# A four-layer transformer kernel on one core: the first tile's turnings moved ahead of the last output products at the layer boundaries

## The reference

```python
# first block (layers 0, 1): a norm behind the part too
x = x + gt[:, None, :] * rmsnorm(o, g_post)
h = modulate(rmsnorm(x, g_pre), shift, scale)     # h * (1 + scale) + shift
# second block (layers 2, 3)
h = h + g1 * y
a = rmsnorm_2(h, norm) * (1.0 + sc) + sh
```

## Time and profile before

| | us |
|---|---|
| three runs, median (lowest, highest) | 1362.74 (1361.14, 1364.23) |
| the profiled execution | 1363.81 |
| its span (first to last instruction) | 1362.5 |
| TensorE busy in it | 1298.8 (95%) |
| VectorE busy | 1079.2 (79%) |
| ScalarE busy | 770.0 (57%) |

### The profile page before, as it was taken

How to read it: one execution, slowest core, us unless ns; L and a number is a source line. 1 busy time by engine, 2 the same in 40 slices (tenths; PEclk the granted TensorE clock), 3 DMA queues, 4 the chain that set the end, 5 groups by cost and what they waited for, 6 DMA issues and landing times.

```text
span 1362.5 us, 20647 instructions
## 1 busy us (share of the span) xinstructions
PE 1298.8 (95%) x8024; PEld 1135.3 (83%) x8024; DVE 1079.2 (79%) x1691; ACT 770.0 (57%) x1330; POOL 45.2 (3%) x74
## 2 busy tenths in 40 slices
PE   4999899999999889999989999899999899999998
PEld 3998799998798689998777786688888799788887
DVE  6887788887868788779887886798887887777753
ACT  4755745553856575554574666765543644655541
POOL 0022000000014100000000000000000000000000
PEclk8999899999999999999999999999999999899999
DMA  9966587679577544667934433167788576347550
GB/s 375 374 233 226 184 300 280 265 292 375 187 297 280 187 158 171 253 249 267 354 124 155 171 121 127 63 267 306 292 297 342 211 285 255 126 184 292 225 203 37
DMA packets 46738, 319.96 MB, mean 235 GB/s; under 512 B 5216, under 2 KB 5808, under 8 KB 9648
## 3 DMA queue, kind: packets, MB, share of 16 engines
q1 hardware_dynamic: 46640, 318.63, 61.7%
HBM read 317.51 MB, written 1.10 MB: 234 GB/s over the span
## 4 chain that ended last, share of the span: by engine, by line
PE 65%; DVE 17%; DMA 7%; ACT 6%; issue 4%; SPq 0%; POOL 0%; ACTq 0%; DVEq 0%
PE mat L663 10%; DVE wlo L1724 7%; PE mat L736 7%; PE mat L738 6%; PE mat L740 6%; PE mat L698 5%; PE mat L662 5%; PE mat L700 5%; PE mat L699 5%; DVE raw L1751 3%; ACT whi L1217 3%; DMA raw<-in_down 2%; DMA raw<-in_mod 2%; PE mat L1106 2%; PE mat L1108 2%
## 5 line engine op out<-in xcount | busy, mean ns | idle before, releaser
L1724 DVE TENSOR_TENSOR wlo<-raw,whi 128x1024 fp32r<-128x1024 f32 x393 | 475.8, 1223 | 140.5 <-ACT whi L1217 137.6
L1217 ACT ACTIVATE whi<-raw 128x1024 fp32r<-128x1024 f32 x393 | 406.1, 1052 | 195.8 <-DMA raw<-in_down 75.3
L698 PE MATMUL mat<-hHL,whi 128*128 128x256 f32 x1080 | 308.4, 286 | 3.9 <-DVE tmp L2271 2.8
L699 PE MATMUL mat<-hHL,whi 128*128 128x256 f32 x1080 | 305.5, 283 | 0.0
L700 PE MATMUL mat<-hHL,wlo 128*128 128x256 f32 x1080 | 305.5, 283 | 0.0
L1751 DVE SCALAR_TENSOR_TENSOR raw<-raw,cB 128x1024 f32<-128x1024 f32 x180 | 218.1, 1222 | 12.6 <-DMA raw<-in_mod 12.3
L663 PE MATMUL mat<-hHL,whi 128*128 128x512 f32 x616 | 221.4, 399 | 0.0
L698 PEld LDWEIGHTS mat<-hHL,whi 128*128 128x128 f32 x1080 | 207.1, 192 | 8.9 <-DVE tmp L2271 4.3
L699 PEld LDWEIGHTS mat<-hHL,whi 128*128 128x128 f32 x1080 | 207.1, 192 | 0.1
L700 PEld LDWEIGHTS mat<-hHL,wlo 128*128 128x128 f32 x1080 | 207.1, 192 | 0.0
L662 PE MATMUL mat<-hHL,wlo 128*128 128x256 f32 x616 | 172.8, 281 | 0.0
(11 more groups left out here) (237 smaller groups left out, 1872.8 us busy)
## 6 DMA issues: line engine op xcount, KB each, us to landing
raw<-in_mod SPq DMA_DIRECT2D x89, 1024.0 KB, 5.6
raw<-in_qkv SPq DMA_DIRECT2D x46, 1024.0 KB, 6.9
raw<-in_gate SPq DMA_DIRECT2D x44, 1024.0 KB, 5.2
raw<-in_up SPq DMA_DIRECT2D x44, 1024.0 KB, 4.9
raw<-in_down SPq DMA_DIRECT2D x44, 1024.0 KB, 5.9
raw<-in_wo SPq DMA_DIRECT2D x16, 1024.0 KB, 5.0
begin<-in_mod SPq DMA_DIRECT2D x6, 1024.0 KB, 17.0
gtb<-gates SPq DMA_DIRECT2D x8, 512.0 KB, 7.1
```

The lines of the kernel that those rows point to most:

```text
L698: pe.matmul(o, wh[:, k, :], hH[:, k, :], start=(k == 0), stop=False)
L699: pe.matmul(o, wh[:, k, :], hL[:, k, :], start=False, stop=False)
L1217: act.activation(whi[:, n % NSPL, :], raw[:, f % NRAW, 1024 * h:1024 * h + 1024], ACT.Copy).then_inc(s_hi, 1)
L1724: dve.tensor_tensor(out=wlo[:, n % NSPL, :], in0=raw[:, f % NRAW, 1024 * h:1024 * h + 1024], in1=whi[:, n % NSPL, :].bitcast(f32), op=ALU. ...
```

## The change

The number in `TURNED_AHEAD` says how many items of the last product's list still stand behind tile 0's eight turnings, in boundaries 1 and 3 (one item, three matmuls) and 6 and 7 (two items, six). In boundary 5 the turnings stay behind the product. In all five the turnings of tile 0 are counted in three steps (pair 0, pair 1, pairs 2 and 3) instead of two; pair 1 of tile 0 goes from ScalarE, bank 4, to VectorE, bank 5; and the steps of ScalarE and VectorE are put in another order, one for b = 1 and 3, one for 6 and 7, one for 5.

```diff
+        TURNED_AHEAD = {1: 1, 3: 1, 6: 2, 7: 2}
...
             if t == 0:
-                return "act" if p < 2 else "dve"
+                return "act" if p == 0 else "dve"
...
             if t == 0:
-                return (4, 256 * p) if p < 2 else (7, 256 * (p - 2))
+                return (4 + p, 0) if p < 2 else (7, 256 * (p - 2))
...
+            order = list(order)
+            for behind, (k, t, *half) in zip(range(len(order) - 1, -1, -1), order):
...
+                if turned_ahead in TURNED_AHEAD and behind == TURNED_AHEAD[turned_ahead]:
+                    first_turned(turned_ahead)
                 yield k, t
...
+        def first_turned(b):
+            for first, last in ((0, 0), (1, 1), (2, 3)):
+                transposes(b, 0, first, last)
+
         def tensor_boundary(b):
-            transposes(b, 0, 0, 1)
-            transposes(b, 0, 2, 3)
+            if b not in TURNED_AHEAD:
+                first_turned(b)
...
             if low:
                 scalar_square(b, "o", 1, 0)
+                scalar_pair(b, 0, 0)
                 scalar_square(b, "o", 1, 1)
+                scalar_high(b, 0, 0, 1)
+                scalar_square(b, "x", 1, 0)
+                scalar_square(b, "x", 1, 1)
+                scalar_high(b, 0, 2)
+                scalar_pair(b, 1, 0, 1)
+            elif b == 5:
+                scalar_square(b, "x", 1, 0)
+                scalar_square(b, "x", 1, 1)
+                scalar_pair(b, 0, 0)
+                scalar_high(b, 0, 0)
+                scalar_pair(b, 1, 0)
+                scalar_high(b, 0, 1)
+                scalar_pair(b, 1, 1)
+                scalar_high(b, 0, 2)
+            else:
                 scalar_pair(b, 0, 0)
                 scalar_square(b, "x", 1, 0)
-            else:
-                scalar_square(b, "x", 1, 0)
-                scalar_pair(b, 0, 0)
-            scalar_square(b, "x", 1, 1)
-            scalar_pair(b, 0, 1)
-            scalar_high(b, 0, 0, 1, 2)
-            scalar_pair(b, 1, 0, 1)
+                scalar_high(b, 0, 0)
+                scalar_square(b, "x", 1, 1)
+                scalar_high(b, 0, 1, 2)
+                scalar_pair(b, 1, 0, 1)
             scalar_high(b, 0, 3)
...
                 vector_scale(b, 0)
                 vector_gated(b, 1, 0)
+                vector_pair(b, 0, 1)
+                vector_pair(b, 0, 2)
                 vector_gated(b, 1, 1)
...
+                if b != 5:
+                    vector_scale(b, 0)
                 vector_gated(b, 1, 0)
                 vector_added(b, 1, 0)
-                vector_scale(b, 0)
+                if b != 5:
+                    vector_pair(b, 0, 1)
+                    vector_pair(b, 0, 2)
                 vector_gated(b, 1, 1)
                 vector_added(b, 1, 1)
-            vector_pair(b, 0, 2)
-            vector_pair(b, 0, 3)
-            vector_scale(b, 1)
-            vector_low(b, 0, 0, 1)
-            for p in range(2):
-                vector_pair(b, 1, p)
-                vector_low(b, 1, p)
+            if b == 5:
+                vector_scale(b, 0)
+                vector_pair(b, 0, 1)
+                vector_scale(b, 1)
+                vector_pair(b, 1, 0)
+                vector_low(b, 0, 0)
+                vector_low(b, 1, 0)
+                vector_pair(b, 0, 2)
+                vector_pair(b, 1, 1)
+                vector_low(b, 0, 1)
+                vector_low(b, 1, 1)
+                vector_pair(b, 0, 3)
+            else:
+                vector_pair(b, 0, 3)
+                vector_low(b, 0, 0, 1)
+                vector_scale(b, 1)
+                for p in range(2):
+                    vector_pair(b, 1, p)
+                    vector_low(b, 1, p)
             vector_low(b, 0, 2, 3)
```

More of the change, by code:

```diff
@@ L423, in pair_bank, with high_order, low_order, taken_order @@
             if t == 0:
-                return (4, 256 * p) if p < 2 else (7, 256 * (p - 2))
+                return (4 + p, 0) if p < 2 else (7, 256 * (p - 2))
             return (2 * p + copy, 0) if p < 2 else (7, 256 * (p - 2))
         PAIRS = [(0, p) for p in range(4)] + [(1, p) for p in range(4)]
+        def high_order(b):
+            if b in BY_TILE:
+                return PAIRS
+            if b == 5:
+                return [(0, 0), (1, 0), (0, 1), (1, 1), (0, 2), (0, 3), (1, 2), (1, 3)]
+            return [(0, 0), (0, 1), (0, 2), (1, 0), (1, 1), (0, 3), (1, 2), (1, 3)]
+        def low_order(b):
+            if b in BY_TILE:
+                return PAIRS
+            if b == 5:
+                return [(0, 0), (1, 0), (0, 1), (1, 1), (0, 2), (0, 3), (1, 2), (1, 3)]
+            return [(0, 0), (0, 1), (1, 0), (1, 1), (0, 2), (0, 3), (1, 2), (1, 3)]
+        def taken_order(b):
+            return [(0, 1), (1, 0), (0, 2), (1, 1), (0, 3)] if b == 5 else PAIRS
         SQ, POW, ROW, PROD = {}, {}, {}, {}
@@ L457, in build @@
                 rows = ["b00", "b01", "c00", "c01", "xn00", "xn01", "b10", "b11", "c10", "c11", "xn10", "xn11"]
+            elif b == 5:
+                rows = ["b00", "c00", "b01", "c01", "b10", "c10", "b11", "c11", "xn00", "xn01", "xn10", "xn11"]
             else:
-                rows = ["b00", "c00", "b01", "c01", "b10", "c10", "xn00", "xn01", "b11", "c11", "xn10", "xn11"]
+                rows = ["b00", "c00", "b01", "c01", "xn00", "xn01", "b10", "c10", "b11", "c11", "xn10", "xn11"]
             for name in rows:
@@ L471, in build @@
                     TMA[b, t, p] = len(TMA) + 1
-                else:
+            for t, p in taken_order(b):
+                if pair_by(b, t, p) != "act":
                     TMD[b, t, p] = len(TMD) + 1
-            for t, p in PAIRS if by_tile else [(0, 0), (0, 1), (0, 2), (1, 0), (1, 1), (0, 3), (1, 2), (1, 3)]:
+            for t, p in high_order(b):
                 HH[b, t, p] = len(HH) + 1
-            for t, p in PAIRS if by_tile else [(0, 0), (0, 1), (1, 0), (1, 1), (0, 2), (0, 3), (1, 2), (1, 3)]:
+            for t, p in low_order(b):
                 HL[b, t, p] = len(HL) + 1
@@ L480, in build @@
                     TR[b, t, p, 0], TR[b, t, p, 1] = len(TR) + 1, len(TR) + 2
-                elif p % 2 or (by_tile and (t, p) == (0, 1)):
+                elif p % 2 or (t, p) == (0, 1 if by_tile else 0):
                     TR[b, t, p] = len(TR) + 1
@@ L721, in token_product, with token_parts @@
                 pass
-        def token_parts(halves, nk, order, sH, sL, ready, then=None):
-            for k, t, *half in order:
+        def token_parts(halves, nk, order, sH, sL, ready, then=None, turned_ahead=None):
+            order = list(order)
+            for behind, (k, t, *half) in zip(range(len(order) - 1, -1, -1), order):
                 n = halves[k]
@@ L824, in tensor_program @@
                         [(k, 0, c) for c in range(2) for k in (6, 7)] + [(k, 1, c) for c in range(2) for k in range(4, 8)]
-                wo = token_parts(range(HALF["wo", l, 0], HALF["wo", l, 0] + KT), KT, order, oH, oL, o_ready)
+                wo = token_parts(range(HALF["wo", l, 0], HALF["wo", l, 0] + KT), KT, order, oH, oL, o_ready,
+                                 turned_ahead=2 * l + 1)
                 if l < 2:
@@ L866, in tensor_program @@
                     gate_row(l, 5)
-                token_product(range(HALF["down", l, 0], HALF["down", l, 0] + FT), FT, token_order(FT, [1] * 9 + [2], 1 if l < 2 else 2), aH, aL, a_ready)
+                token_product(range(HALF["down", l, 0], HALF["down", l, 0] + FT), FT, token_order(FT, [1] * 9 + [2], 1 if l < 2 else 2), aH, aL, a_ready,
+                              turned_ahead=2 * l + 2)
                 if l < 2:
```

3 lines of the change are left out of this document (2 added, 1 removed).

## The result

| | us |
|---|---|
| before, median of 7 runs (lowest, highest) | 1362.24 (1360.52, 1365.90) |
| changed, median of 7 runs (lowest, highest) | 1370.68 (1366.95, 1375.32) |
| ratio, 95% interval | 1.0068 (1.0052 to 1.0084) |
| profiled execution of the changed kernel, its span | 1369.94, 1368.6 |

The change makes the kernel slower by 0.68% (0.0068 x 1362.2 = 9.3 us, 7.1 to 11.4). The forecast was 1371.4.

The account below looks back on a forecast made before the run. TensorE's chain of waits bounds the kernel, with each boundary's path starting at tile 1's last chunk. 1.6 + 1.3 + 2.6 + 2 x (0.9 + 0.7) = 8.7 on 1362.74 gives 1371.4 us, range 1365.0 to 1376.0.

Parts of the forecast that it names:

- (1): b = 6 and 7: eight turnings ahead of six products make the last chunk end later, +0.9 us each.
- (2): b = 6 and 7: VectorE's low part ahead of tile 1's scaling waits for ScalarE's high part, +0.7 us each.
- (3): b = 1: three products behind the turnings end later, 0.8 us of it existing slack; +1.6 us.
- (4): b = 3: three products behind the turnings end later, with less slack than b = 1; +1.3 us.
- (5): Behind tile 1's scaling: highs and lows moved ahead give back up to 0.5 us per boundary; taken as 0.
- (6): b = 5: VectorE's awaited pair, now last of eleven steps, delays the product; +2.6 us, 3.0 at half clock.
- (7): Every boundary: group 1's pair moves from ScalarE to VectorE, 0.7 us of VectorE each, inside the other sums.
- The clock: 6 us behind each first product: 5.7 us lost now in all; change taken as 0, reach 4 either side.
- B: VectorE and ScalarE hold the boundaries, not the last chunk; lows leave the path, -2.5 us, 1360.2 us; 6%.
- D: b = 5: its wait costs nothing, another pair holds TensorE; +6.1 us in all, 1368.8 us; 12%.
- C: Clock luck behind the boundaries: 6.7 - 5.7 = +1.0 us, 1363.7 us, no difference to be told; 9%.
- E: Clock at its worst behind the boundaries: 8.7 + 7.8 us, 1379.2 us; 8%.

Follow-up runs that it names:

- the late products alone: Kernel before with eight idle turnings added ahead of the last product items, VectorE's and ScalarE's orders untouched; ratio 1.0015 (1.0001 to 1.0029).
- the filled kernel: Kernel before with idle turnings nobody reads filling TensorE's idle stretch ahead of tile 1's turnings; ratio 1.0007 (0.9991 to 1.0023).

## Why the prediction was right

By its own steps, with the length of the boundary as the ruler:

- **(1) The turnings push the last products**, +0.9 in b = 6 and 7. Right: 0.79 from the first turning to the product behind, and 0.9 each where only that was done to the kernel before.
- **(2) The new wait**, +0.7. Right: the wait is there as described (0.68 idle), it delays the scaling by 0.65, and at the same clock of the turnings 0.65 reached the product in b = 6. Together with (1) the scaling of tile 1 starts 1.55 later in b = 7 (7.23 for 5.68); forecast 1.6.
- **(3), (4) b = 1 and 3**, +1.6 and +1.3. Measured +1.61 and +1.14. TensorE idled 1.24 ahead of the turnings in b = 1 (forecast 1.2), and ScalarE took the chunk as it ended. In b = 3 the scaling starts 1.37 later and 0.23 come back behind it.
- **(5) What comes back**, taken as 0. In this profile that was the wrong one of two named ends in b = 6 and 7: with the low parts gone from there, VectorE's first pair starts 0.74 behind the first turning (1178.77 to 1179.51), and the stretch from the scaling to the product is 2.66 to 2.68 where it was 3.07 to 3.09. 0.4 of the 0.5 came back, so these boundaries grew by 1.13 and 1.16, not 1.6. In b = 1, at half clock, nothing came back, as the step said. And in b = 6 of two other profiles with the same code, whose turnings took 2.82, nothing came back either: the stretch was 3.10 and the boundary had grown by 1.56 and 1.55. So both ends of the step are real, and the clock that the turnings are granted chooses between them.
- **(6) b = 5**, +2.6, or 3.0 with turnings at half clock. Measured +3.47: the mechanism was right to the row, the size too small. Eight turnings of tile 0 took 1.97 instead of 1.09, the first pair of each tile waited 0.81 for turnings, and the last four took 1.12. The step should have taken its slow-clock end, since TensorE idles 1.98 directly ahead. That number depends on the profile: the experiments without turnings ahead and with the low part moved have 9.89 there with the same code, +3.01, which is the step's slow-clock end.
- **(7)** is inside these sums; VectorE's busy time grew by 3.1 us over the span, five pairs of 0.7 being 3.5.

The sum is 8.5 where 8.7 was forecast; +0.9 in b = 5 and about -0.9 in b = 6 and 7 cancelled, with -0.2 in b = 3. The mechanisms were right; that the sum came within 0.2 is luck, since the terms move by 0.4 to 0.5 each with the clock. **The clock** was taken as 0 in sum, and was: 5.6 lost for 5.7. That too is chance, with 1.3 to 7.4 in the other profiles without filling. The profiled spans differ by only 6.1 because the stretches between the boundaries differ by -2.4 in sum (+2.4 from the last gate piece of layer 0 to b = 3, -1.4 behind b = 3, -2.0 between b = 5 and 6, -1.7 behind b = 7, +0.2 elsewhere, rounded); over seven runs the medians differ by 8.4, and the ratio says 9.3.

**The rivals.** B fell with the late products alone, D with b = 5 put back. C and E did not come true; but the filled kernel shows that both rested on a wrong price. They counted every lost TensorE cycle behind a boundary as time, and with nearly all of them gone the kernel was no faster; why not, the stages show only in part. The reach of 4 us to either side was therefore too generous for the clock. It covered instead a spread that the prediction had not named, that of the stretches which wait for weights.

## What to carry to other kernels

Work moved ahead of the last product on an in-order engine isn't free because its input is ready: ask first whether the path starts at that product's end, by the distance from its end to the instruction that takes it (0.04 to 0.11 us here meant no slack, 0.8 meant slack), and count the moved work in full if it does. In an order written out by hand, follow for each step who waits for it: one pair put last in eleven steps held TensorE 3.6 us and cost 2.0 of boundary, and a low part in front of a scaling cost 0.65. Before a difference of a few tenths between two profiles is read as the edit's, compare the clock of the same instructions in both: here twelve turnings took 1.53 to 2.82, and that alone moved a boundary by 0.4. A low granted clock cost nothing behind b = 1 and about 2 us behind b = 7; look at which stage follows before paying for a warm clock.

## What the runs showed of the hardware

- The clock is held when an idle stretch is filled with turnings that nobody reads: granted 1.00 behind all five boundaries, for 0.55 to 0.95. Over the whole run the mean granted clock rose from 0.987 to 0.996, and the time did not fall. In the stage behind b = 1, a clock of 0.76 over its first 6 us and one of 1.00 gave the same length (132.3 and 132.2 us).
- In b = 5 eight fp32 turnings took 1.97 us in the changed kernel's profile, at the low level (1.2 GHz), and 1.09 at the high one before; twelve took 2.82 and 1.53. Profiles of the same code differ in this way, and a boundary's length with them by up to 0.5 us.
- A stretch of some 187 us, in which ScalarE waits for transfers and TensorE for split weights, varied by 6 us from profile to profile (185.0 to 190.9), as much as most of the edits tried here moved the time. A single pair of spans is no measure of such a change; the sum over the boundaries was one to within some tenths each.
